# A two-layer transformer block on one core: attention scores of two 64-wide heads as two 64-row matmuls, units in pairs

## The chip, the cores and the metric

One core of one Trainium2 chip. The time is the device time of one launch in microseconds; the kernel before has three runs. The engines are called PE (TensorE: matmuls and transposes; PEld is its weight loads), DVE (VectorE), ACT (ScalarE), POOL (GpSimd) and SP (it only issues DMAs here).

## What is computed

512 latent tokens and 256 context tokens, 1024 wide, go through two layers in fp32. Each layer normalises and modulates the tokens, projects them once, and runs four groups of four heads side by side: A full attention with two key heads, B latent attention (keys 96 wide), C a window of 128 keys to either side with a sink, D a neighbourhood with a learned bias; all of them also look at the 256 context keys. Then an output projection, a residual, and a mixture of 64 experts of which each token takes 8.

```python
def _dense_block_attn(q, k, v, scale):
    ...
        s = jnp.einsum("bhgqd,bhkd->bhgqk", qi, k, preferred_element_type=jnp.float32) * scale
        p = jax.nn.softmax(s, axis=-1).astype(v.dtype)
        return jnp.einsum("bhgqk,bhkd->bhgqd", p, v)
...
    for l in range(DEPTH):
        with_ctx = l < DEPTH - 1
        ...
        mix = jnp.concatenate([oa, ob, ow, on], axis=-1) @ w_out[l]
        x = x + g1 * _rms_norm(mix, post_mix_g[l])
        ...
        f = _moe(tokens, router_w[l], router_b[l], exp_w_gate[l], exp_w_up[l], exp_w_down[l], ...)
```

In layer 0 the context tokens are updated too (they attend to context keys alone), in layer 1 not.

## The kernel before

`build` calls, for each layer, `norm_in`, four times `mixer` (groups A, B, C, D), `project_out`, then `route`, `experts` and `ffn_residual`. Each is a block with one instruction list per engine, written out by hand; between blocks all engines meet. Semaphores (`Signal`) order the engines within a block, and each engine works through its list in order. In the profile the tensors of a mixer carry its layer and group in their name: PR_0A, KT_1D.

A `mixer` has two parts. In the first, PE projects the six token tiles of 128 (`project`, L550) and turns queries and keys (`turn`, L571), so that QT and KT hold the width of a head in the partitions. In the second it works off **units**: one head for one tile of 128 queries, in the order head by head, tile by tile. There are 24 units in layer 0 (6 tiles: 4 latent, 2 context) and 16 in layer 1. For each unit:

- `scores` (PE, L581 and L582): queries against up to 512 latent keys and against 256 context keys, into one of two areas of PSUM, `pp[u % 2]`. Context units have the second product alone.
- `maximum` (DVE, L788; D first subtracts its bias, L782; C its masks, L785 and L787, and takes the sink in, L791): the scores are negated, so it is a minimum.
- `exps` (ACT, L670): exponentials and their sum, into PR.
- `turn_probs` (PE, L589): six transposes of 128 columns.
- two copies from PSUM into PT: the latent part on ACT (L680), the context part on DVE (L820).
- `values` (PE, L597): six products with V; behind them, in some units, two tiny products (L603) that finish a **piece** of the modulation vector.
- `divide` (DVE, L801 and L807, in C also L799; L804 for the piece): the result into o_tok.

The heads of A, C and D are 64 wide. KT holds two key heads one above the other, in partitions 0 to 63 and 64 to 127, and QT holds each query head in the half of its key head, the other half being zero (memset, L714). So a product over 128 rows gives the scores of one head. B has rows 0 to 95 filled and the rest zero.

The pieces are the work of POOL (`piece`, L512 to L515): 12 per mixer in layer 0 and 8 in layer 1, each 9.3 us long, multiplying and adding weights that SP loads two at a time (L498). Piece j goes with unit `unit_of[j]`, that is units 1, 3, 5 and so on up to the last; `values` of that unit waits for it. After 8 pieces POOL needs a slot that `values` has read.

The order on the engines, with u the unit:

```python
for u in range(NU):          # PE (between: scores(0) first, values(NU - 1) last)
    scores(u + 1); values(u - 1); turn_probs(u)
for u in range(NU):          # ACT, after exps(0)
    exps(u + 1); copy_latent(u)
for u in range(NU):          # DVE, after maximum(0)
    maximum(u + 1); divide(u - 1); copy_context(u)
```

`scores(u)` waits for the exponentials of u - 2, `turn_probs(u)` for those of u and for `divide(u - 2)`.

Of the kernel before, what the change touches and what calls it, by code (L numbers as in the profile page):

```python
# [27 lines left out]
P = 128  # L28
# [3 lines left out]
SEQ, CTX = 512, 256  # L32
LT, CT = SEQ // P, CTX // P
NT = LT + CT
HD = 64
# [9 lines left out]
NROW = NT * P  # L45
# [355 lines left out]
def mixer(v, l, g, nt, hT, wg, o_tok):  # L401
# [5 lines left out]
    isA, isB, isC, isD = (name == x for x in "ABCD")  # L407
# [12 lines left out]
    s_sc, s_max, s_exp, s_pt = S("scores"), S("negated_maximum"), S("exponentials"), S("probs_turned")  # L420
    s_pa, s_pd, s_pv, s_o, s_sx = S("probs_by_act"), S("probs_by_dve"), S("weighted_values"), S("out_written"), S("sink_exp")

    units = [(h, q) for h in range(4) for q in range(nt)]
    NU = len(units)

    def lo(u):

        q = units[u][1]
        if q >= LT:
            return 512  # L430
        if isC:
            return 512 - P * (min(q + 1, LT - 1) - max(q - 1, 0) + 1)
        return 0
# [17 lines left out]
    NP, NA = len(pieces), 8  # L451
# [3 lines left out]
    s_aw, s_as, s_acc = [S("ada_loaded0"), S("ada_loaded1")], S("ada_step"), S("ada_summed")  # L455
    s_mr, s_pad = S("mod_columns"), S("padded")

    steps, counts = [], []
    local = [sum(units[w][1] < LT for w in range(u + 1)) for u in range(NU)]

    with ExitStack() as scope:
# [20 lines left out]
        pp = [v.banks(0, 2), v.banks(2, 4)]  # L482
        tq, tk = ps[:, 4, :], ps[:, 5, :]

        with nc.Block() as block:  # L485
# [54 lines left out]
            @block.tensor  # L540
            def _(pe):
                def project(i):

                    s_rows.wait(pe, i - 1)
                    if not isB:
                        s_v.wait(pe, i - 1)
                    a = 0 if has_q[i] else kv0
                    for c0, c1 in ((a, min(W, 512)), (512, W)):
                        for k in range(KD if c1 > c0 else 0):
                            last = pe.matmul(pp[i % 2][:, c0:c1], hT[:, k, i * P:(i + 1) * P], wg[g % 2][:, k, c0:c1],  # L550
                                             start=(k == 0), stop=(k == KD - 1))
                    last.then_inc(s_proj.sem, 1)

                def latent(i):

                    s_cn.wait(pe, i + 1)
                    pe.transpose(ps[:, 7, 0:P], cn[:, i % 2, :], v.ident).then_inc(s_ct.sem, 1)
                    s_ce.wait(pe, i + 1)
                    s_kn.wait(pe, i)
                    pe.matmul(ps[:, 6, :], cT[:, i % 2, :], wup[:, :], start=True, stop=True).then_inc(s_up.sem, 1)  # L560

                def turn(i):
                    s_rows.wait(pe, i + 1)
                    if isB:
                        s_kn.wait(pe, i + 1)
                    s_qe.wait(pe, nq[i])
                    s_ke.wait(pe, i)
                    for j in range(0 if has_q[i] else NQ, NQ + NK):
                        dst, c = (tq, j) if j < NQ else (tk, j - NQ)
                        src = R[:, i % 2, j * KP:(j + 1) * KP]  # L570
                        last = pe.transpose(dst[0:KP, c * P:(c + 1) * P], src, v.ident)  # L571
                    last.then_inc(s_t.sem, 1)

                def scores(u):
                    s, q = units[u]
                    s_exp.wait(pe, u - 1)
                    kvp = s if isB else s // 2 if isD else 0
                    a, k0 = lo(u), key_tile(u, lo(u) // P) * P
                    lhs = QT[:, s, q * P:(q + 1) * P]
                    if a < 512:  # L580
                        pe.matmul(pp[u % 2][:, a:512], lhs, KT[:, kvp, k0:k0 + 512 - a], start=True, stop=True)  # L581
                    pe.matmul(pp[u % 2][:, 512:768], lhs, KT[:, kvp, SEQ:NROW], start=True, stop=True).then_inc(s_sc.sem, 1)  # L582

                def turn_probs(u):
                    s_exp.wait(pe, u + 1)
                    s_o.wait(pe, u - 1)
                    b = 4 + 2 * (u % 2)
                    for c in range(lo(u) // P, 6):
                        last = pe.transpose(ps[:, b + c // 4, (c % 4) * P:(c % 4 + 1) * P], PR[:, u % 2, c * P:(c + 1) * P], v.ident)  # L589
                    last.then_inc(s_pt.sem, 1)  # L590

                def values(u):
                    s_pa.wait(pe, local[u])
                    s_pd.wait(pe, u + 1)
                    c0 = kv_of(units[u][0]) * HD
                    for c in range(lo(u) // P, 6):
                        last = pe.matmul(ps[:, 5 + 2 * (u % 2), 256:256 + HD], PT[:, u % 2, c * P:(c + 1) * P],  # L597
                                         V[:, key_tile(u, c), c0:c0 + HD], start=(c == lo(u) // P), stop=(c == 5))
                    if u in piece_of:
                        j = piece_of[u]  # L600
                        s_acc.wait(pe, j + 1)
                        for c in range(2):
                            last = pe.matmul(ps[:, 5 + 2 * (u % 2), 320 + c:321 + c], acc[:, j % NA, c, :], v.ones[:, :],  # L603
                                             start=True, stop=True)
                    last.then_inc(s_pv.sem, 1)

                s_w.wait(pe, 16)
                if isB:
                    s_wup.wait(pe, 16)
                project(0)  # L610
                for i in range(NT):
                    if i + 1 < NT:
                        project(i + 1)
                    if isB:
                        latent(i)
                    turn(i)

                s_qe.wait(pe, nq[NT])
                s_ke.wait(pe, NT)
                s_pad.wait(pe, 2)  # L620
                if not isB:
                    s_v.wait(pe, NT)
                scores(0)
                for u in range(NU):
                    if u + 1 < NU:
                        scores(u + 1)
                    if u:
                        values(u - 1)
                    turn_probs(u)
                values(NU - 1)  # L630

            @block.scalar
            def _(act):
# [29 lines left out]
                def exps(u):  # L663
                    s_max.wait(act, u + 1)
                    s_pt.wait(act, u - 1)
                    a = lo(u)
                    if isC:
                        act.activation(st[:, 3, u:u + 1], small[:, S_SINK + units[u][0]:S_SINK + units[u][0] + 1], ACT.Exp,
                                       bias=st[:, 1, u:u + 1])
                    act.activation(PR[:, u % 2, a:768], pp[u % 2][:, a:768], ACT.Exp, bias=st[:, 1, u:u + 1], scale=-1.0,  # L670
                                   accum_out=st[:, 2, u:u + 1]).then_inc(s_exp.sem, 1)

                exps(0)
                for u in range(NU):
                    if u + 1 < NU:
                        exps(u + 1)
                    if lo(u) < 512:
                        s_pt.wait(act, u + 1)
                        s_pv.wait(act, u - 1)
                        act.copy(PT[:, u % 2, lo(u):512], ps[:, 4 + 2 * (u % 2), lo(u):512]).then_inc(s_pa.sem, 1)  # L680

            @block.vector
            def _(dve):
                n = [0]
# [23 lines left out]
                if isB:  # L708
                    dve.memset(QT[KP:P, :, :], 0.0).then_inc(s_pad.sem, 1)
                    dve.memset(KT[KP:P, :, :], 0.0).then_inc(s_pad.sem, 1)  # L710
                else:
                    for side in range(2):
                        rest = QT[(1 - side) * HD:(2 - side) * HD, :, :].rearrange("p (j s) n -> p j s n", s=2)
                        dve.memset(rest[:, :, side, :], 0.0).then_inc(s_pad.sem, 1)  # L714
                for i in range(NT):
                    tok = slice(i * P, (i + 1) * P)
                    pr = pp[i % 2]
# [92 lines left out]
                if isC:  # L810
                    step(dve.tensor_scalar(nsink[:, :], small[:, S_SINK:S_SINK + 4], -1.0, None, ALU.mult))
                maximum(0)
                for u in range(NU):
                    if u + 1 < NU:
                        maximum(u + 1)
                    if u:
                        divide(u - 1)
                    s_pt.wait(dve, u + 1)
                    s_pv.wait(dve, u - 1)
                    dve.tensor_copy(PT[:, u % 2, 512:768], ps[:, 5 + 2 * (u % 2), 0:256]).then_inc(s_pd.sem, 1)  # L820
                divide(NU - 1)
                steps.append(n[0])

# [4 lines left out]
        s.stage_over(k)  # L828
    for j in range(2):
        s_aw[j].stage_over(16 * ((NP + 1 - j) // 2))  # L830
    for s, k in ((s_as, counts[0]), (s_acc, NP), (s_pad, 2), (s_mr, NP)):
        s.stage_over(k)
    if not isB:
        s_v.stage_over(NT)
# [852 lines left out]
```

## Time and profile before

| | |
|---|---|
| runs | 3464.82, 3468.37, 3480.79 us (median 3468.37) |
| span of the profiled execution | 3472.4 us (the page gives no time of its own beside it) |
| PE, DVE, ACT, POOL busy | 87%, 37%, 18%, 33% |
| attention stretches of the eight mixers | 484.3 us of span in sum: PE 450.6 busy, DVE 304.2, POOL 389.1 |
| the eight mixers, projections included | 1070 us |
| experts | most of the rest |

The page's busy shares are averages over stages of different kind: the 142 expert blocks alone hold most of PE's time. What the change touches lies in eight stretches of 49 to 80 us each, so they are read by windows, and the engines' interplay by the timeline. A busy time is the sum of instruction durations; the number in brackets behind a row of the timeline is how long the engine stood idle before it, and what released it. An "x2" joins instructions of the same kind that follow each other. Each fp32 product is two LDWEIGHTS and two MATMUL records.

### The profile page before, as it was taken

How to read it: one execution, taken by the hardware profiler on the slowest of the kernel's cores; microseconds unless marked ns; L12 is line 12 of the kernel's file. 1: busy time of each engine (PE TensorE's matmuls, PEld its weight loads, DVE VectorE, ACT ScalarE, POOL GpSimd, SP SyncE). 2: the span in 40 equal slices, each digit the busy share in tenths (PEclk: the TensorE clock that was granted, in tenths of full speed). 3: DMA queues.
4: the chain of work that ended last, by engine and by line, in shares of the span. 5: the costliest groups of instructions: out<-in, count | busy, mean ns of one | idle time of the engine just before them, and what ended most of it. 6: DMA issues, size and time to landing. Idle time of an engine off the chain costs nothing. (4 is left out here: it accounts for less than half of the span.)

```text
span 3472.4 us, 54592 instructions
## 1 busy us (share of the span) xinstructions
PE 3025.3 (87%) x17979; PEld 2267.7 (65%) x17980; DVE 1300.4 (37%) x3937; ACT 617.2 (18%) x1376; POOL 1162.9 (33%) x1009
## 2 busy tenths in 40 slices
PE   6688979988899999989994698899789999999995
PEld 5365655636577777777773466666457777777774
DVE  5643461524333333323334644524322332233223
ACT  1122231310111111111113122212111111111111
POOL 0766798500121222212222637672111221222122
PEclk9898999997999999999997898999799999999998
DMA  6121212103589888898884211221359999988995
GB/s 218 31 70 37 85 49 96 62 27 112 214 252 322 263 251 287 284 306 272 286 276 141 67 53 31 85 88 39 114 184 312 300 310 295 300 273 245 300 304 161
DMA packets 199258, 642.71 MB, mean 185 GB/s; under 512 B 23296, under 2 KB 117760, under 8 KB 165632
## 3 DMA queue, kind: packets, MB, share of 16 engines
q1 hardware_dynamic: 157264, 520.86, 41.2%
q0 software_dynamic: 41904, 120.67, 16.9%
q8 instruction: 53, 0.87, 0.1%
q14 instruction: 37, 0.30, 0.0%
HBM read 589.19 MB, written 89.03 MB: 195 GB/s over the span
## 5 line engine op out<-in xcount | busy, mean ns | idle before, releaser
L1389 PEld LDWEIGHTS ps<-xT,wgu 128*128 128x128 f32 x9088 | 1033.3, 192 | 116.0 <-issue 115.2
L1389 PE MATMUL ps<-xT,wgu 128*128 128x128 f32 x9088 | 1048.1, 276 | 26.4 <-DVE xT L1473 24.2
L1337 POOL DMA_INDIRECT X<-h_rows,gix x146 | 149.2, 1022 | 1300.8 <-DVE wc L1476 659.5
L1396 PE MATMUL ps<-wd,hidden 128*128 128x512 f32 x1136 | 525.8, 606 | 0.0
L550 PE MATMUL ps<-w_in,hT 128*128 128x512 f32 (+3 forms) x1152 | 396.9, 505 | 15.6 <-PEq L485 4.3
L1396 PEld LDWEIGHTS ps<-wd,hidden 128*128 128x128 f32 x1136 | 209.3, 194 | 215.1 <-issue 212.3
L550 PEld LDWEIGHTS ps<-w_in,hT 128*128 128x128 f32 x1152 | 213.2, 203 | 184.9 <-issue 177.4
L1485 DVE TENSOR_TENSOR hidden<-silu,ps 128x128 f32<-128x128 f32 x284 | 81.5, 287 | 596.7 <-ACT silu L1441 595.4
L1356 POOL DMA_INDIRECT ffn_rows<-Y,six x142 | 226.4, 1595 | 170.8 <-ACT Y L1446 147.7
L1382 PE MATMUL ps<-cst,X 128*128 128x128 f32 x1152 | 162.3, 286 | 99.4 <-DMA X<-h_rows,gix 99.1
L1441 ACT ACTIVATE silu<-ps 128x128 f32<-128x128 f32 x284 | 78.7, 277 | 902.3 <-PE ps L1389 902.3
L1382 PEld LDWEIGHTS ps<-cst,X 128*128 128x128 f32 x1152 | 128.2, 144 | 106.5 <-DMA X<-h_rows,gix 106.2
L1446 ACT ACTIVATE Y<-ps,wc 128x512 f32<-128x512 f32 x142 | 97.6, 687 | 442.0 <-PE ps L1396 402.4
L1487 DVE COPY six<-gix 128x1 uint32<-128x1 uint32 x142 | 21.8, 153 | 344.2 <-DMA ffn_rows<-Y,six 344.0
L1498 DVE TENSOR_SCALAR Y<-ps,wc 128x512 f32<-128x512 f32 x142 | 106.4, 749 | 111.3 <-PE ps L1396 111.3
L906 PE MATMUL ps<-w_in,oT 128*128 128x512 f32 x320 | 139.3, 594 | 0.0
L1459 DVE TENSOR_SCALAR mark<-csth,cur 128x128 f16<-128x128 f16 x736 | 137.0, 271 | 5.2
L1435 ACT COPY xT<-ps 128x512 f32<-128x512 f32 x144 | 84.2, 585 | 246.3 <-PE ps L1382 246.3
L1455 DVE TENSOR_SCALAR cur<-gm,cst 128x6 f32 (+1 forms) x146 | 47.1, 322 | 168.1 <-issue 168.1
L906 PEld LDWEIGHTS ps<-w_in,oT 128*128 128x128 f32 x320 | 60.6, 191 | 73.0 <-issue 73.0
L1473 DVE COPY xT<-ps 128x512 f32<-128x512 f32 x144 | 98.0, 680 | 10.0 <-PE ps L1382 10.0
L930 POOL TENSOR_TENSOR mss<-mss,half 128x1 f32<-128x1 f32 x10 | 5.5, 548 | 204.7 <-DVE mss L954 204.7
(447 smaller groups left out, 3652.4 us busy)
## 6 DMA issues: line engine op xcount, KB each, us to landing
wgu<-in_exp_gu SPq DMA_DIRECT2D x128, 2048.0 KB, 8.9
wd<-in_exp_d SPq DMA_DIRECT2D x128, 1024.0 KB, 7.8
ada_start<-in_ada_w SPq DMA_DIRECT2D x8, 1024.0 KB, 9.7
w_in<-in_w_in SPq DMA_DIRECT2D x4, 2048.0 KB, 8.2
w_in<-in_w_out SPq DMA_DIRECT2D x4, 2048.0 KB, 11.1
aw_0A<-in_ada_w SPq DMA_DIRECT2D x12, 512.0 KB, 3.8
aw_0B<-in_ada_w SPq DMA_DIRECT2D x12, 512.0 KB, 3.9
w_in<-in_w_in SPq DMA_DIRECT2D x2, 3072.0 KB, 10.6
```

The source lines that it names most:

```text
L550: last = pe.matmul(pp[i % 2][:, c0:c1], hT[:, k, i * P:(i + 1) * P], wg[g % 2][:, k, c0:c1], start=(k == 0), stop=(k == KD - 1))
L906: last = pe.matmul(ps[:, 2 * (i % 2) + n, :], oT[:, i % 2, k, :], w[n][:, k, 0:512], start=(k == 0), stop=(k == KD - 1))
L1337: pool.indirect_dma_start(out=X[j][:, :], out_offset=None, in_=v.h2_dram, in_offset=bass.IndirectOffsetOnAxis(ap=gix[j][:, 0:1], axis=0), ...
L1356: pool.indirect_dma_start(out=v.acc_dram, out_offset=bass.IndirectOffsetOnAxis(ap=six[j][:, 0:1], axis=0), in_=Y[j][:, :], in_offset=None, ...
L1382: last = pe.transpose(ps[:, 3 + k // 4, (k % 4) * P:(k % 4 + 1) * P], X[j][:, k * P:(k + 1) * P], v.ident)
L1389: last = pe.matmul(ps[:, f, h * P:(h + 1) * P], wgu[w][:, k, h * FD + f * P:h * FD + (f + 1) * P], xT[:, k, :], start=(k == 0), stop=(k == ...
L1396: last = pe.matmul(ps[:, 5 + c, :], G[:, f, :], wd[w][:, f, c * 512:(c + 1) * 512], start=(f == 0), stop=(f == 1))
L1435: act.copy(xT[:, 0:4, :].rearrange("p k c -> p (k c)"), ps[:, 3, :]).then_inc(x_act, 1)
L1446: act.activation(Y[j][:, 0:512], ps[:, 5, :], ACT.Copy, scale=wc[j][:, 0:1]).then_inc(y_act, 1)
L1459: last = dve.tensor_scalar(mark[:, t, :], csth[:, H_IOTA:H_IOTA + P], cur[:, t:t + 1], None, ALU.is_equal)
L1473: dve.tensor_copy(xT[:, 4:8, :].rearrange("p k c -> p (k c)"), ps[:, 4, :]).then_inc(x_dve, 1)
L1498: dve.tensor_scalar(Y[j][:, 512:D], ps[:, 6, :], wc[j][:, 0:1], None, ALU.mult).then_inc(y_dve, 1)
```

## The change

Units are taken in pairs: heads 2j and 2j + 1 for the same tile. `scores_of_two` issues the wide product of both heads and then the narrow product of both; each reads only the 64 partitions that its head fills (B still reads 128). The two heads are in different halves of the array's rows and write to different areas of PSUM. QT's other halves are no longer set to zero, and PE's wait for the memsets goes, except in B. The order of the three engines within the attention part is new for all four groups.

```diff
-    units = [(h, q) for h in range(4) for q in range(nt)]
+    units = [(2 * j + s, q) for j in range(2) for q in range(nt) for s in range(2)]
...
-                def scores(u):
-                    s, q = units[u]
-                    s_exp.wait(pe, u - 1)
-                    kvp = s if isB else s // 2 if isD else 0
+                def scores_of_two(u):
+
+                    s_exp.wait(pe, u)
                     a, k0 = lo(u), key_tile(u, lo(u) // P) * P
-                    lhs = QT[:, s, q * P:(q + 1) * P]
-                    if a < 512:
-                        pe.matmul(pp[u % 2][:, a:512], lhs, KT[:, kvp, k0:k0 + 512 - a], start=True, stop=True)
-                    pe.matmul(pp[u % 2][:, 512:768], lhs, KT[:, kvp, SEQ:NROW], start=True, stop=True).then_inc(s_sc.sem, 1)
+                    for c0, c1, k in ((a, 512, k0), (512, 768, SEQ)):
+                        for w in range(2 if c0 < c1 else 0):
+                            s, q = units[u + w]
+                            side = slice(0, P) if isB else slice((s % 2) * HD, (s % 2 + 1) * HD)
+                            ins = pe.matmul(pp[w][:, c0:c1], QT[side, s, q * P:(q + 1) * P],
+                                            KT[side, s if isB else s // 2 if isD else 0, k:k + c1 - c0], start=True, stop=True)
+                            if c0 == 512:
+                                ins.then_inc(s_sc.sem, 1)
...
-                s_pad.wait(pe, 2)
-                if not isB:
+                if isB:
+                    s_pad.wait(pe, 2)
+                else:
                     s_v.wait(pe, NT)
-                scores(0)
-                for u in range(NU):
-                    if u + 1 < NU:
-                        scores(u + 1)
-                    if u:
-                        values(u - 1)
+                scores_of_two(0)
+                for u in range(0, NU, 2):
+                    if u + 2 < NU:
+                        scores_of_two(u + 2)
                     turn_probs(u)
-                values(NU - 1)
+                    turn_probs(u + 1)
+                    values(u)
+                    values(u + 1)
...
                 exps(0)
+                exps(1)
                 for u in range(NU):
-                    if u + 1 < NU:
-                        exps(u + 1)
                     if lo(u) < 512:
                         s_pt.wait(act, u + 1)
                         s_pv.wait(act, u - 1)
                         act.copy(PT[:, u % 2, lo(u):512], ps[:, 4 + 2 * (u % 2), lo(u):512]).then_inc(s_pa.sem, 1)
+                    if u % 2 == 1 and u + 1 < NU:
+                        exps(u + 1)
+                        exps(u + 2)
...
-                else:
-                    for side in range(2):
-                        rest = QT[(1 - side) * HD:(2 - side) * HD, :, :].rearrange("p (j s) n -> p j s n", s=2)
-                        dve.memset(rest[:, :, side, :], 0.0).then_inc(s_pad.sem, 1)
...
                 maximum(0)
+                maximum(1)
                 for u in range(NU):
-                    if u + 1 < NU:
-                        maximum(u + 1)
-                    if u:
+                    if u % 2 == 0 and u:
+                        divide(u - 2)
                         divide(u - 1)
+                    if u + 2 < NU:
+                        maximum(u + 2)
                     s_pt.wait(dve, u + 1)
                     s_pv.wait(dve, u - 1)
                     dve.tensor_copy(PT[:, u % 2, 512:768], ps[:, 5 + 2 * (u % 2), 0:256]).then_inc(s_pd.sem, 1)
+                divide(NU - 2)
                 divide(NU - 1)
```

On PE, in the midst of 1D's attention (scores L581 and L582, values L597, piece L603, turns L589), two units stand before as

```order
L581 MATMUL ps<-KT_1D,QT_1D 128x512
L582 MATMUL ps<-KT_1D,QT_1D 128x256
L597 MATMUL ps<-V_1D,PT_1D 128x64 x6
L603 MATMUL ps<-ones,aacc_1D 128x1 x2
L589 MATMUL ps<-cst,PR_1D 128x128 x6
L581 MATMUL ps<-KT_1D,QT_1D 128x512
L582 MATMUL ps<-KT_1D,QT_1D 128x256
L597 MATMUL ps<-V_1D,PT_1D 128x64 x6
L589 MATMUL ps<-cst,PR_1D 128x128 x6
```

and in the changed kernel, where L582 is both score products, L592 the turns, L600 the values and L606 the piece, as

```order
L582 MATMUL ps<-KT_1D,QT_1D 128x512 x2
L582 MATMUL ps<-KT_1D,QT_1D 128x256 x2
L592 MATMUL ps<-cst,PR_1D 128x128 x12
L600 MATMUL ps<-V_1D,PT_1D 128x64 x12
L606 MATMUL ps<-ones,aacc_1D 128x1 x2
```

The values of a unit stood one unit behind its turns, with the next scores between them; now both follow at once, and nothing stands between the second turns and the values.

On DVE at the same place, before (bias L782, minimum L788, L801 to L807 the division, L820 the copy), two units:

```order
L782 TENSOR_TENSOR ps<-ps,TD_1D 128x512
L788 TENSOR_REDUCE st_1D<-ps 128x1
L801 RECIPROCAL st_1D<-st_1D 128x1
L804 TENSOR_SCALAR mod_raw<-ps,small 128x2
L807 TENSOR_SCALAR o_tok<-ps,st_1D 128x64
L820 COPY PT_1D<-ps 128x256
L782 TENSOR_TENSOR ps<-ps,TD_1D 128x512
L788 TENSOR_REDUCE st_1D<-ps 128x1
L801 RECIPROCAL st_1D<-st_1D 128x1
L807 TENSOR_SCALAR o_tok<-ps,st_1D 128x64
L820 COPY PT_1D<-ps 128x256
```

and in the changed kernel (bias L784, minimum L790, division L803 to L809, copy L824):

```order
L803 RECIPROCAL st_1D<-st_1D 128x1
L809 TENSOR_SCALAR o_tok<-ps,st_1D 128x64
L803 RECIPROCAL st_1D<-st_1D 128x1
L806 TENSOR_SCALAR mod_raw<-ps,small 128x2
L809 TENSOR_SCALAR o_tok<-ps,st_1D 128x64
L784 TENSOR_TENSOR ps<-ps,TD_1D 128x512
L790 TENSOR_REDUCE st_1D<-ps 128x1
L824 COPY PT_1D<-ps 128x256
L784 TENSOR_TENSOR ps<-ps,TD_1D 128x512
L790 TENSOR_REDUCE st_1D<-ps 128x1
L824 COPY PT_1D<-ps 128x256
```

The divisions of a pair stand together ahead; the copy of the second unit stands behind the bias and minimum of the second unit of the next pair.

## Rows read from the trace of the kernel before

**Rows 1.** The page's head.

```profile
span 3472.4 us, 54592 instructions
```

**Rows 2.** Stretches (attention of 0A, 0C, 1A, 1D): PE, PEld, DVE, ACT, POOL busy; PEclk.

```profile
150.00:216.00 66.00, 63.94 (x407) 50.41 (x408) 35.21 (x90) 28.09 (x60) 61.61 (x57) 0.96 0.20 57
447.70:515.00 67.30, 53.47 (x344) 42.20 (x345) 53.25 (x156) 25.68 (x79) 62.67 (x60) 0.97 0.19 56
1979.60:2035.00 55.40, 54.58 (x350) 44.09 (x350) 28.53 (x66) 23.93 (x47) 39.40 (x37) 0.96 0.10 29
2338.50:2395.00 56.50, 54.07 (x350) 42.46 (x350) 38.71 (x82) 23.53 (x47) 28.53 (x28) 1.00 0.07 20
```

**Rows 3.** Timeline of 1A: start, length, engine, line, what [idle before, releaser].

```profile
1993.04 1.02 PE L581 MATMUL ps<-KT_1A,QT_1A 128*128 128x512 f32 x2
1994.34 1.45 PE L597 MATMUL ps<-V_1A,PT_1A 128*128 128x64 f32 x12
1994.54 0.96 DVE L788 TENSOR_REDUCE st_1A<-ps 128x1 f32<-128x768 f32 x1 [0.87 <-PE ps L582]
1995.53 0.90 ACT L670 ACTIVATE PR_1A<-ps,st_1A 128x768 f32<-128x768 f32 x1 [1.70 <-DVE st_1A L788]
1995.62 0.83 PE L589 MATMUL ps<-cst,PR_1A 128*128 128x128 f32 x6
1996.28 1.02 PE L581 MATMUL ps<-KT_1A,QT_1A 128*128 128x512 f32 x2
1996.33 0.19 ACT L670 ACTIVATION_READ_ACCUMULATOR PR_1A<-ps,st_1A 128x1 f32 x1
1996.48 0.58 ACT L680 COPY PT_1A<-ps 128x512 f32<-128x512 f32 x1
1996.48 0.42 DVE L820 COPY PT_1A<-ps 128x256 f32<-128x256 f32 x1 [0.18 <-PE ps L589]
1998.86 0.56 PE L603 MATMUL ps<-ones,aacc_1A 128*128 128x1 f32 x4
1999.97 0.60 PE L581 MATMUL ps<-KT_1A,QT_1A 128*128 128x512 f32 x1
```

**Rows 4.** Timeline of 1D, two units.

```profile
2354.09 1.02 PE L581 MATMUL ps<-KT_1D,QT_1D 128*128 128x512 f32 x2
2355.58 0.70 DVE L782 TENSOR_TENSOR ps<-ps,TD_1D 128x512 f32<-128x512 f32 x1 [0.82 <-PE ps L582]
2355.59 1.42 PEld L597 LDWEIGHTS ps<-V_1D,PT_1D 128*128 128x128 f32 x12 [0.45 <-ACT PT_1D L680]
2361.33 1.02 PE L581 MATMUL ps<-KT_1D,QT_1D 128*128 128x512 f32 x2
```

**Rows 5.** Timeline: the last piece on POOL and on PE, 0A to 0D.

```profile
228.18 0.45 POOL L515 TENSOR_TENSOR aacc_0A<-atmp_0A 128x128 f32<-128x128 f32 x1
228.68 1.02 PE L603 MATMUL ps<-ones,aacc_0A 128*128 128x1 f32 x4 [2.33 <-POOL aacc_0A L515]
396.17 0.45 POOL L515 TENSOR_TENSOR aacc_0B<-atmp_0B 128x128 f32<-128x128 f32 x1
397.08 0.96 PE L603 MATMUL ps<-ones,aacc_0B 128*128 128x1 f32 x4
523.71 0.45 POOL L515 TENSOR_TENSOR aacc_0C<-atmp_0C 128x128 f32<-128x128 f32 x1
525.52 0.96 PE L603 MATMUL ps<-ones,aacc_0C 128*128 128x1 f32 x4
654.51 0.45 POOL L515 TENSOR_TENSOR aacc_0D<-atmp_0D 128x128 f32<-128x128 f32 x1
676.97 0.96 PE L603 MATMUL ps<-ones,aacc_0D 128*128 128x1 f32 x4
```

**Rows 6.** Timeline: start of 0A's mixer on DVE.

```profile
72.82 1.34 DVE L714 MEMSET QT_0A<- 64x1536 f32 x1 [0.79 <-PEq L294]
```

**Rows 7.** Timeline: first scores of 1A.

```profile
1979.66 2.04 PE L581 MATMUL ps<-KT_1A,QT_1A 128*128 128x512 f32 x2 [0.43 <-DVE KT_1A L772]
```

More of the change, by code:

```diff
@@ L830, in mixer @@
         s_aw[j].stage_over(16 * ((NP + 1 - j) // 2))
-    for s, k in ((s_as, counts[0]), (s_acc, NP), (s_pad, 2), (s_mr, NP)):
+    for s, k in ((s_as, counts[0]), (s_acc, NP), (s_pad, 2 if isB else 0), (s_mr, NP)):
         s.stage_over(k)
```

## The prediction

> **What bounds the kernel now.** The page gives the span of the profiled execution [rows 1], 3472.4 us, and no time outside it; the median of the runs is 3468.37. The sum below is a difference against the profiled execution, which stands 0.1% above the median. Only the attention part of eight mixers is touched: 0A to 0D with 24 units each (a unit is one head of one 128-token tile), 1A to 1D with 16. The table by stretches [rows 2] shows PE busy for 98 to 99% of 0A's and 1A's attention, 96% of 1D's, and 79% of 0C's, where DVE has as much work. So PE seems to be the bound, and the timeline of 1A [rows 3] shows a unit's parts: the scores take 1.30 us (1993.04 to 1994.34), the weighted values 1.28 (to 1995.62), the six turns of the probabilities 0.66 (to 1996.28). Two units take 6.93 (1993.04 to 1999.97): twice 3.24, and 0.45 for the piece of modulation that every second unit adds. In 1D [rows 4] two units take 7.24 (2354.09 to 2361.33), since the weights of the values wait 0.45 for ACT.
>
> Two things beside PE matter. First POOL: it sums the modulation pieces, and the last unit of each mixer waits for the last of them. The ends of the mixers [rows 5] show 0A's last piece on POOL done at 228.63 and PE waiting 2.33 us for it; in 0B POOL is done at 396.62, PE's last product starts at 397.08; in 0C 524.16 and 525.52; only in 0D (654.96 against 676.97) and in layer 1 has POOL long been done. POOL's work is unchanged and hardly waits for attention. Second, the chain around PE: minimum on DVE 1.50 us after the scores start, exponentials, turn, two copies 0.86 after the turn starts, values [rows 3]. Before, each step has one unit's work as cover.
>
> **The change, part by part.**
>
> *The memsets* of QT's empty halves [rows 6] are dropped from DVE: 2 x 1.34 us while PE projects; the first result of that projection is there 8 us later. Worth 0.
>
> *The scores in halves of the array* (A, C, D). The arithmetic is as before, 4 matmul records per unit (two passes per product), 0.43 us for 512 columns, 0.22 for 256. No row shows two matmuls in different halves, so the price of a pair's scores lies between 2.60 us (one after the other, 2 x 1.30) and 1.30 (completely together). I take a value between: the two passes of one head use the same half and must follow each other, and matmuls start in the order of the program; so only the second pass of one head runs beside the first pass of the other. That gives 3 x 0.43 for the wide products, in whose last 0.43 the first head's two narrow passes fit, and 2 x 0.22 more: 1.73.
>
> *The new order, A.* PE does scores of both next units, two turns, two values; DVE does minimum, copy, minimum, copy; ACT both copies, then both exponentials. Counted from the start of the scores: first minimum 1.50 to 2.46; turns 1.73 to 3.05; copies can start at 2.59 and 3.25. DVE: copy to 3.01, second minimum to 4.00, second copy to 4.45. ACT: copies to 3.84, exponentials (0.90 + 0.19 each) to 6.04. PE: values 3.3 to 4.6, second values to 5.9, piece to 6.35. So a pair takes 6.35 where it took 6.93: 0.58 less, eight pairs 4.6. The start is dearer: the second pair's scores and the first turns wait for two minima and the second exponential, which ends 4.6 after the first scores start (1.50 + 0.99 + 0.99 + 1.12), while PE has 1.73 of work: 2.9 idle. Before, the first turns waited for one exponential, which ends at 3.6 with 2.6 of scores ahead: 1.0 idle. The 1.9 more, less 0.87 for the cheaper scores and what is saved at the last pair, I take as 0.6. 1A: -4.0.
>
> *B* keeps 128 rows and gets only the order. The first minimum starts at 2.35 (three products stand ahead of it), turns 2.60 to 3.92, ACT's copy ends at 4.05, values from 4.2, the end at 7.23: 0.30 more than 6.93. 1B: +2.4.
>
> *D* has the bias subtraction (0.70, 0.73 with its gap [rows 4]) ahead of each minimum, and the copy that the second values wait for stands behind both: 1.50 + 0.73 + 0.99 + 0.45 + 0.73 + 0.99 + 0.45 = 5.84, then 0.1 to restart, values 1.30, piece 0.45: 7.69. That is 0.45 more than 7.24 in the seven cycles from pair to pair, so 1D is +3. In 0D the latent pairs lose as much, the four context pairs gain (their scores shrink from 0.86 to 0.65, and they stand together): 0.
>
> *C* is between: DVE has masks, a second small minimum and one step more per unit. I take +1 for 1C (ends -2 and +4, the gain of A and the loss of D).
>
> *0A, 0B, 0C.* POOL's end stays: 0A cannot end earlier (0), 0B by 0.5 at most (0), 0C by 1.4 at most (-1). Were POOL faster, the cover of 0A's gain would be gone and some 4 us would appear.
>
> *The clock.* The first scores of 1A run at 1.2 GHz (2.04 us for two passes, against 1.02) [rows 7]; four tiny matmuls at the end of 0A take 1.02 against 0.56 [rows 3, 5], after PE had waited. More waiting at starts and in context pairs may keep the lower level a little longer: +1 over all.
>
> Sum over 0A to 0D and 1A to 1D: 0 + 0 - 1 + 0 - 4.0 + 2.4 + 1 + 3, and 1 for the clock: **+2**, with some 8 us either way if 0.1 us per pair is wrong in my chains (80 pairs). Against the median that is **3470 us**. What PE saves (0.87 us in most of the 60 pairs of A, C and D) goes to three places: POOL's end, the queue on DVE, and the starts.
>
> The Trainium skill ("TensorE: Matmul & The Clock Gate", Part 3) says that small matmuls in different row groups start some 4 ns apart and run together; no run here shows it. By it a pair's scores would take 1.30; the A pair would then be held by ACT's exponentials at 6.2, so the sum hardly moves.
>
> **The rivals.**
>
> 1. *The halves don't run together* (slower). Then the pair's scores take 2.60, the first minimum starts at 2.35, A pairs take 7.2 like B, D pairs 5.84 + 0.85 + 1.85 = 8.5. 1A +2, 1B +2, 1C +1, 0C -1, 0D +6 (eight latent pairs at +1.3, context pairs giving some back), 1D +9, clock +1: +20, 3488. For it: fp32 runs in two passes, and no row shows a pass beside another. Against it: different rows, different banks of PSUM. It decides from the point at which the overlap is under a third.
>
> 2. *Going from 128 rows to 64 and back empties the array.* The last of a row of 512-wide matmuls is shown 0.16 us longer than its spacing (1.02 for two at 0.43) [rows 3], so two switches cost 0.32 per pair. In the 36 pairs of 0D, 1A, 1C and 1D that is 12 at most, about 7 where DVE's chain covers one of the two: 3476. The Trainium skill ("TensorEngine Tiling (Array Packing)", Key Properties) states that a change of tiling mode drains TensorE. No run here shows it; it speaks against the change.
>
> 3. *PE alone decides* (faster). If the chain through DVE has more slack than I count, what PE saves is the gain: 8 x 0.87 each in 1A and 1D, 8 x 0.75 in 1C, about 8 in 0D: 28, so 3440. For it: 98% busy [rows 2]. Against it: in 1D the cycle is over 7.24 with PE busy for 6.9.
>
> 4. *The clock falls in the midst of attention*, because PE now waits in each pair. A pair of 6 us of PE work then takes some 10: +3 us and more in each of 80 pairs, over 3700. Against it: 0C ran with PE busy 79% at 0.97 [rows 2].
>
> **How the numbers follow.** A measurement of this kernel tells about 0.5% (17 us: under 3451 or over 3486) from no change. The forecast has 0.62, rival 1 0.16, rival 2 0.12, rival 3 0.06, rival 4 0.04. Forecast and rival 2 are the same within 0.5%, and rival 1, at 3488, lies at the bound: a fifth of it counts as same. Faster 0.06, same 0.77, slower 0.17. The range goes from 3457 (the forecast with its chains 8 better and 5 for the spread of the runs) to 3489 (rival 1); it leaves out rivals 3 and 4.
>
> **What would show it.** In the timeline of the changed kernel: scores records of a pair 0.43 apart with the second head's first pass starting with the first head's second; 1A about 4 us shorter with some 6.3 per pair; 1D with 7.6 to 7.7 and PE idle ahead of the second values, waiting for DVE's copy; 1B at 7.2; PE at 0A's last piece waiting 5 us or more for POOL and the mixer ending at the same time as before. D pairs at 7.0 or less, 0A ending early, or B pairs under 6.9 would prove me wrong; scores of 2.6 per pair would prove rival 1.

## The result and the profile after

The changed kernel takes 3498.12 us (median of 4 runs, 3495.89 to 3507.59) against 3474.0 for the kernel before on the same chips: a ratio of 1.0081 (95% interval [1.0056, 1.0106], as in all brackets behind a ratio below), 0.8% slower. The profiled execution has a span of 3505.4 us against 3472.4 [rows 1]. It is the slowest of the four runs: it shows 33.0 us more, where the medians differ by 24.1. The mean granted clock of the whole kernel is 0.923 to 0.925 in all four; the runs of the kernel before beside the first experiments have 0.936 to 0.941. The page:

```profile
span 3505.4 us, 54574 instructions
PE 3036.0 (87%) x17979; PEld 2279.0 (65%) x17980; DVE 1272.2 (36%) x3925; ACT 614.1 (18%) x1376; POOL 1164.4 (33%) x1009
PEclk9888979896899999999997898889799999999998
```

The stretches from the first scores to the last piece, after (columns as in [rows 2], whose stretches are shorter; 0A to 0D, then 1A to 1D):

```profile
150.50:229.70 79.20, 66.95 (x463) 53.86 (x464) 37.61 (x105) 29.24 (x65) 73.25 (x68) 0.87 0.16 47
324.80:405.00 80.20, 74.92 (x463) 59.63 (x464) 37.88 (x105) 28.01 (x64) 70.20 (x66) 0.95 0.16 47
454.80:538.90 84.10, 71.92 (x392) 58.05 (x392) 59.64 (x177) 28.02 (x88) 71.35 (x67) 0.70 0.16 45
609.40:693.20 83.80, 69.22 (x464) 56.25 (x464) 48.32 (x121) 28.78 (x64) 54.65 (x51) 0.90 0.11 32
1996.40:2053.10 56.70, 53.55 (x384) 43.68 (x384) 27.83 (x69) 23.70 (x48) 39.40 (x37) 0.90 0.10 29
2135.80:2200.80 65.00, 62.64 (x383) 49.33 (x384) 28.32 (x69) 23.70 (x48) 36.21 (x35) 0.93 0.09 25
2241.30:2307.50 66.20, 57.36 (x311) 47.16 (x311) 44.32 (x125) 22.30 (x64) 44.84 (x43) 0.69 0.11 32
2367.80:2434.80 67.00, 55.38 (x383) 43.87 (x384) 38.17 (x85) 24.57 (x48) 30.46 (x29) 0.92 0.06 17
```

Before, the same eight stretches lasted 550.7 us in sum; now 582.2, which is 31.5 of the span's 33.0. Only 1A is shorter. The column to look at is the granted clock (1.00 is TensorE's full 2.4 GHz, 0.50 its low level of 1.2 GHz): 0.69 and 0.70 in 1C and 0C, where it was 0.98 and 0.96.

All runs in one table: length of each stretch, its clock behind it. There is one profile of each. Where the clock stays high, mixers of equal code agree within about 1 us. Where it falls they do not: 0C with the code of before takes 78.4, 91.1 (c_as_before), 79.2 and 78.3 (the last two rows), and 1C with the changed code 66.2 and, with light POOL, 59.9.

```
                    0A        0B        0C        0D         1A        1B        1C        1D
before           79.2 .93  76.3 .95  78.4 .96  79.7 .97   60.3 .96  60.7 .96  55.0 .98  61.1 1.0
changed          79.2 .87  80.2 .95  84.1 .70  83.8 .90   56.7 .90  65.0 .93  66.2 .69  67.0 .92
order_only       80.3 .95  80.2 .95  81.8 .90  94.2 .88   65.0 .94  64.9 .94  64.0 .89  79.9 .85
halves_only     142.2 .50  75.9 .97 118.0 .50 142.5 .50  118.0 .50  60.7 .96  91.6 .51 117.2 .50
halves_filled    98.1 .96  75.7 .97  92.6 .91 102.4 .92   78.1 .95  60.3 .96  63.9 1.0  77.7 .96
copies_first     79.2 .87  79.6 .95  78.6 .79  79.7 .87   56.7 .90  65.0 .93  57.3 .82  63.1 .89
turns_first      79.3 .87  77.5 .95  91.7 .67  80.1 .87   55.2 .93  61.8 .97  68.1 .70  58.5 .97
c_as_before      79.3 .87  80.2 .95  91.1 .76  82.0 .93   56.6 .90  65.0 .93  55.0 .97  66.9 .90
c_filled         79.3 .87  80.3 .95  78.8 .89  87.0 .85   56.7 .90  65.0 .93  60.3 .92  68.4 .88
light_pool chg.  72.0 .90  80.2 .95  80.5 .76  83.9 .90   55.6 .92  65.0 .94  59.9 .80  71.8 .81
light_pool bef.  76.7 .95  75.0 .97  76.3 .89  80.0 .97   60.7 .96  60.3 .96  54.2 .98  61.1 1.0
best_of_each     79.2 .89  75.7 .97  79.2 .94  77.2 .91   55.1 .93  60.2 .97  54.9 .96  61.3 .92
pieces_moved     74.9 .84  76.3 .95  78.3 .96  77.5 .91   55.1 .93  60.4 .96  53.9 1.0  60.0 .94
```

The timeline of 1A after, PE, one pair:

```profile
2023.54 1.56 PE L582 MATMUL ps<-KT_1A,QT_1A 64*128 64x512 f32 x8
2025.04 1.53 PE L592 MATMUL ps<-cst,PR_1A 128*128 128x128 f32 x12
2026.59 2.89 PE L600 MATMUL ps<-V_1A,PT_1A 128*128 128x64 f32 x24
2029.31 0.56 PE L606 MATMUL ps<-ones,aacc_1A 128*128 128x1 f32 x4
2029.80 1.56 PE L582 MATMUL ps<-KT_1A,QT_1A 64*128 64x512 f32 x8
```

The scores of two units last 1.50 us (2023.54 to 2025.04). The halves run together: 2 x 0.43 + 2 x 0.22 is 1.30, and I put the other 0.20 down to the changes of rows. The Trainium skill ("TensorE: Matmul & The Clock Gate", Part 3) says that matmuls in different row groups run at the same time and start some 4 ns apart. The trace agrees in fp32: the single records of this pair show each pass of the second head 6 to 7 ns behind that of the first. The pair takes 6.26 (2023.54 to 2029.80). In 1D two pairs, PE, the first with its scores at the low clock and the second at the full:

```profile
2390.20 2.81 PE L582 MATMUL ps<-KT_1D,QT_1D 64*128 64x512 f32 x8
2395.20 1.52 PE L600 MATMUL ps<-V_1D,PT_1D 128*128 128x64 f32 x12 [0.34 <-DVE PT_1D L824]
2397.13 1.52 PE L600 MATMUL ps<-V_1D,PT_1D 128*128 128x64 f32 x12 [0.41 <-DVE PT_1D L824]
2398.98 1.56 PE L582 MATMUL ps<-KT_1D,QT_1D 64*128 64x512 f32 x8
2406.51 1.56 PE L582 MATMUL ps<-KT_1D,QT_1D 64*128 64x512 f32 x8
```

8.78 us for the first (2390.20 to 2398.98), 7.53 for the second (7.24 before [rows 4]). In the first pair PE waits for DVE's copy ahead of both values; in the second, the first wait is 0.73 for ACT's copy. At 0A's end PE waits 5.15 us for POOL's last piece (2.33 before [rows 5]):

```profile
229.06 1.01 PE L606 MATMUL ps<-ones,aacc_0A 128*128 128x1 f32 x4 [5.15 <-POOL aacc_0A L515]
```

### The profile page after: what moved, and what is told of

It reads as the page before. It is cut to its first block and busy times, and to the rows that moved or that the text cites. A ratio compares the mean times of both kernels' runs of the same rounds, so it can differ in the third digit from the quotient of the medians.

```text
span 3505.4 us, 54574 instructions
## 1 busy us (share of the span) xinstructions
PE 3036.0 (87%) x17979; PEld 2279.0 (65%) x17980; DVE 1272.2 (36%) x3925; ACT 614.1 (18%) x1376; POOL 1164.4 (33%) x1009
```

## The experiments

Three theories, of which more than one can hold. Theory W (waits): the new waits of PE bring the clock down. Theory H (halves): the 64-row scores do, since they keep less of the array at work. Theory Q (queue): the copy queued behind DVE's minimum holds the values.

**order_only** (`side = slice(0, P)` in `scores_of_two`, memsets kept).

> The changed kernel's order, but the scores of A, C and D again over all 128 rows with QT's other half zero. Theory W (waiting): the clock falls in 0C and 1C because PE stands still in every pair under the new order; then it falls here too, 1C has a mean granted clock near 0.7 and lasts over 64 us from the first scores to the last piece (55.0 before, 66.2 after the change), and the kernel is 30 us or more over the one before. Theory H (halves): it falls because the 64-row scores keep the engine less busy in the chip's eyes; then 1C here has a clock above 0.93 and lasts 56 to 58, and the kernel is about 18 us over the one before (from my chains with the scores in series: 1A +2.4, 1B +2.4, 1C +1, 0D +6, 1D +9, 0C -3). Both: pair scores last 2.6 us, 1A some 62 to 63 us against 60.3 before, 1D some 70 against 61.1.

Measured: 1.0188 [1.0162, 1.0215], 61 us more in the median (W asked for 30 or more, H for 18). 1C has 0.89 and 64.0 us: the new order lowers the clock by itself, but to 0.69 only with the halves. In 1D it is the other way round, 0.85 here and 0.92 with the halves. The pairs' scores last 2.67, as expected. 1D takes 79.9 where I expected 70: its pairs take 8.42 at the full clock, and three in a row have their scores at the low one and take 9.9 to 10.0, though no wait inside them is over 0.47:

```profile
2384.67 2.83 PE L582 MATMUL ps<-KT_1D,QT_1D 128*128 128x512 f32 x8
2393.09 4.41 PE L582 MATMUL ps<-KT_1D,QT_1D 128*128 128x512 f32 x8
2402.98 4.52 PE L582 MATMUL ps<-KT_1D,QT_1D 128*128 128x512 f32 x8
2412.99 4.52 PE L582 MATMUL ps<-KT_1D,QT_1D 128*128 128x512 f32 x8
2422.99 2.83 PE L582 MATMUL ps<-KT_1D,QT_1D 128*128 128x512 f32 x8
```

Shorter scores leave PE more time to wait, so the halves could have worked through the waits. In C the traces speak against it: behind the start, PE's waits in 1C sum to 5.1 us in the changed kernel (none over 0.9) and to 6.7 in the kernel before (up to 1.5, at a clock of 0.98). A slower PE waits less, so this alone is no proof; the next run is.

**halves_only** (the kernel before, `lhs = QT[side, ...]` and `KT[side, ...]` over 64 partitions).

> The order of before, with each unit's scores over the 64 rows its head fills (the two heads not next to each other). Theory H: the clock falls in 1C, 0C and 1D though no wait is added; 1C longer by 5 us or more. Theory W: the clock stays as before (0.96 to 1.00), and each unit costs only the change from 128 to 64 rows and back: 0.12 + 0.2 us as the changed kernel's pairs show around their scores, so 1A and 1D grow by 16 x 0.33 = 5 us each, 0D by up to 8, 1C by 3, 0A to 0C by less since POOL ends them; some +20 us in all. If that price is not paid, +0.

Measured: 1.0906 [1.0876, 1.0935], 310 us more. 1A:

```profile
2138.00:2256.00 118.00, 116.65 (x384) 84.63 (x384) 29.73 (x69) 25.14 (x48) 39.31 (x37) 0.50 0.05 14
```

PE is busy for 99% and yet at 1.2 GHz from end to end; so are all stretches of A, C and D (0.50 and 0.51), and not those of B (0.97 and 0.96), whose code is as before. Nothing but the 64 rows is different. That is H, and far beyond the 5 us that I had asked of it.

**halves_filled** (halves_only, and in `turn_probs` of A, C, D three times `pe.matmul(ps[:, b + 1, 384:512], v.ident, v.ident)`: full-width products whose result nobody reads).

> The old order with 64-row scores (1A 118 us, clock 0.50), with three 128-row products of 128 columns added per unit in A, C and D. If 64-row products merely fail to hold the clock up, the added full-width work brings it back in part: clock above 0.8 and 1A near 16 x (3.46 + 0.33 + 0.66) = 71 us, shorter than 118 although work was added. If they pull it down whatever stands beside them, the clock stays 0.50 and 1A lasts 118 + 21 = 139.

Measured: 3558.61 us in one run, 225 less than halves_only, with 720 more passes of 128 columns (an estimate of 79 us, at half of the 0.22 of a 256-column pass). 1A:

```profile
2030.20:2108.30 78.10, 76.75 (x480) 59.53 (x480) 29.72 (x69) 25.23 (x48) 39.29 (x37) 0.95 0.07 21
```

So 64-row products fail to hold the clock up; full-width work among them brings it back. The changes from 128 rows to 64 and back are all still there, so they alone do not bring it down.

1A takes 78.1 where I expected 71: that sum of 16 units left out the start and the end of the stretch, 4.9 us of the 60.3 before. The run also gives a price for the changes of rows. One unit at the full clock:

```profile
2050.28 0.89 PE L590 MATMUL ps<-cst 128*128 128x128 f32 x6
2051.01 0.82 PE L592 MATMUL ps<-cst,PR_1A 128*128 128x128 f32 x6
2051.75 1.12 PE L582 MATMUL ps<-KT_1A,QT_1A 64*128 64x512 f32 x2
2053.24 1.55 PE L600 MATMUL ps<-V_1A,PT_1A 128*128 128x64 f32 x12
2054.63 0.56 PE L606 MATMUL ps<-ones,aacc_1A 128*128 128x1 f32 x4
2055.05 0.91 PE L590 MATMUL ps<-cst 128*128 128x128 f32 x6
```

Without the added products (0.73) and the piece (0.42) the unit takes 3.62, against 3.24 before [rows 3]: 0.38 more.

**c_filled** (changed kernel, the same three products ahead of the second turns, in C).

> The changed kernel with three 128-row products of 128 columns added ahead of each pair's second turns, in C alone: 0.66 us more work of PE per pair at 2.4 GHz, 5 us in 1C. If the clock is what C lost (H or W), the granted clock in 1C rises from 0.69 to above 0.9 and 1C lasts 62 or less in spite of the added work (66.2 without it). If the clock is only a symptom of waits whose length is set elsewhere, 1C lasts 71 or more.

Measured: 1C 60.3 us at 0.92, 5.9 less with 5 added; 0C 5.3 less at 0.89. So the clock was C's loss. (The added products also fill some of PE's waits, so this run does not tell H from W.) The total, 1.0098 [1.0070, 1.0125], is no better than the changed kernel's: in the profiled run 0D, whose code is unchanged, took 3.2 more at 0.85.

```profile
2231.10:2291.40 60.30, 50.35 (x359) 42.65 (x360) 42.92 (x125) 21.99 (x64) 44.88 (x43) 0.92 0.13 36
```

**c_as_before** (changed kernel with C's order and rows as before).

> The changed kernel with only the C mixers as before (order and 128 rows). If 0C and 1C lose by their own mixture of halves and waits, they last 78 and 55 again and the kernel is 17 us under the changed one (5.7 + 11.2), some 3481. If the clock in C falls because of what runs ahead of it, they stay above 82 and 62.

Measured: 1.0061 [1.0038, 1.0084], some 7 us under the changed kernel's ratio where I expected 17, and the two intervals overlap. 1C is back at 55.0. But 0C, whose program is now the one before, took 91.1 at 0.76. Its clock can fall with 128-row scores and without any change of its own; why it did here is open. So the 5.7 us that 0C lost in the changed kernel cannot be put down to its own halves with certainty.

**copies_first** (DVE: `maximum` of the second unit behind `tensor_copy`).

> The changed kernel with DVE doing both context copies of a pair ahead of the second minimum of the next pair. Theory Q (the queue on DVE holds the second values): 1D's cycle falls from 7.53 to some 6.9 us, 1D to 61 to 62 us from first scores to last piece (67.0 in the changed kernel, 61.1 before), 0D by some 4, 1C by 2 or more; in sum 12 us or more less than the changed kernel. Against it: if the clock alone is what was lost, the waits only move to ACT's exponentials and the gain is under 5 us.

Measured: 1.0043 [1.0023, 1.0062]. 1D's pairs take 6.95 at the full clock (expected 6.9), and both values follow each other without a wait: Q holds. 0D and 1D are 4 us shorter; 1D, at 63.1, stays over the 61 to 62 expected, since one pair is at the low clock. 1C is 9 us shorter with its clock at 0.82 instead of 0.69, so part of that is the clock and not the queue. One edit in DVE's order gives back about half of the loss, by the two ratios; their intervals just touch.

**turns_first** (PE: turns, then `scores_of_two(u + 2)`, then values; DVE: copies, then both minima).

> The changed kernel with the turns of a pair ahead of the scores of the next pair, so that the scores stand between the turns and the values as cover for the copies, and both copies ahead of both minima on DVE. Theory Q: no wait of PE ahead of the values; 1D some 2 us under before, 1A 5 under (55), 0D 5 under; about 12 us less than the changed kernel at equal clock. Theory W adds: with fewer waits of PE the clock in 1C stays above 0.9 and another 8 to 12 us come back. Theory H: 1C's clock stays near 0.7.

Measured: 1.0063 [1.0036, 1.0089], which the intervals do not tell from the changed kernel. 1A (55.2) and 1D (58.5, pairs 6.85) are as expected. 0D is not: 80.1, no better than before, where I expected 5 less. C, at 0.67 and 0.70, took 13 more than before. That does not settle W, because the edit did not take C's waits away: it moved them. In 1C PE now waits for divisions ahead of the turns, 7.9 us in sum against 5.1 in the changed kernel, and for up to 2.16 at a time:

```profile
2245.27 0.74 PE L592 MATMUL ps<-cst,PR_1C 128*128 128x128 f32 x5 [2.16 <-DVE o_tok L809]
2271.91 1.30 PE L592 MATMUL ps<-cst,PR_1C 128*128 128x128 f32 x5 [2.11 <-DVE o_tok L809]
```

**best_of_each** (A and D as in turns_first, B and C as before).

> A and D in pairs with 64-row scores and the turns ahead of the next scores, B and C exactly as before. By the runs so far 1A lasts 55.2 (60.3 before), 1D 58.5 (61.1), 0D about 80 (79.7), B and C as before, 0A held by the last piece: 8 us under the kernel before, some 3466, which the interval may not tell from it. If C's fall of the clock spills over from A and B and is not C's own, 1C stays above 60 and nothing is won.

Measured: 0.9977 [0.9959, 0.9996], 12 runs, 8 us less in the median, as expected: a gain of 0.2% that the interval just tells from nothing. Inside it the parts fell otherwise: 0D took 77.2 (expected 80), 1D 61.3 at 0.92 (expected 58.5). Both C mixers kept their clock (0.94, 0.96) behind the paired A.

**light_pool_before, light_pool_changed** (without the two additions `tmp[:, 0:half] + tmp[:, half:2 * half]`; the modulation is then another, tokens are routed otherwise, so only the mixers compare; one run each).

> The kernel before with the same additions on POOL left out. Its 0A waited 2.33 us for the last piece, so 0A lasts 76 to 77 instead of 79.2. Together with the run on the changed kernel this gives what the change is worth in 0A once POOL is out of the way: 2 to 3 us by this reckoning, 4 to 5 by 1A's example (twice eight pairs alike); nothing if 0A is held by something else.

> The changed kernel with POOL's two intermediate additions per piece left out (part of the modulation sum is missing), so that a piece takes about half as long and no mixer waits for the last one. If POOL's last piece is what ends 0A (5.15 us of waiting there), 0A lasts 73 to 75 us from first scores to last piece instead of 79.2; 0B and 0C change by under 1 us at equal clock; layer 1 not at all.

Measured: 0A 76.7 before and 72.0 changed. With POOL light the change is worth 4.7 us in 0A, with POOL as it is nothing. 0A of the changed kernel came out 1 us under the 73 to 75 expected. 0C fell by 3.6 at 0.76, where I expected under 1 at equal clock, and 1D took 71.8 at 0.81, 4.8 more than in the changed kernel: with the same program on PE and DVE, the clock of C and D moved their times by more than the steps that I had forecast there.

**best_with_pieces_moved** (best_of_each with `share = (11, 12, 12, 13)` pieces for layer 0: one of 0A's pieces goes to 0D).

> The best-of-each kernel with one of 0A's twelve pieces moved to 0D, where POOL is done 20 us early. If POOL ends 0A, 0A gets 4 to 5 us shorter (75) and 0D stays; some 4 us under the best-of-each kernel, 12 under the one before (3460). If PE would be no earlier, 0A stays 79.

Measured: 3454.46 us, 0.9955 [0.9933, 0.9977]; 0A 74.9 (expected 75) and 0D 77.5, as in best_of_each. It beats both kernels, the one before by 0.45%.

## Why the prediction was wrong

The forecast was 3470, no change, in 3457 to 3489; measured 3498, slower by 0.8%. Term by term (us, stretches of the profiles):

```
            0A     0B     0C     0D     1A     1B     1C     1D
forecast     0      0     -1      0   -4.0   +2.4     +1     +3    and +1 for the clock
measured     0   +3.9   +5.7   +4.1   -3.6   +4.3  +11.2   +5.9
```

- ***The clock*, "+1 over all", is the step that failed.** 1C and 0C lost 11.2 and 5.7 where I had +1 and -1. In c_filled a clock of 0.92 and 0.89 instead of 0.69 and 0.70 gives back 5.9 and 5.3 in spite of added work. In 1D, of +5.9, the full-clock pairs explain some 2 (seven times 0.29), two pairs with scores at 1.2 GHz like the one above another 2.5, and the rest is the start, whose second scores run at 1.2 GHz too. I took the clock of 0C, 0.97 at 79% busy, as proof that a PE with waits keeps it, in rival 4 too. That row was of 128-row work in the old order; with 64 rows the busy share no longer speaks for the clock, as halves_only shows (99% busy, 0.50). Rival 4 had the right mechanism. Its reason, the waits, is at most part of it: in order_only the new order alone brings 1D to 0.85 and 1C to 0.89. Its size (every pair of all mixers) was wrong. How much of C's fall in the changed kernel is due to the rows and how much to the order stays open, and 0C in c_as_before fell with neither.
- *0B and 0D* I put at 0. For 0B I had a chain of +0.30 a pair and did not use it, as if POOL's end were a lid with time under it for PE. But PE's last product stood only 0.46 behind POOL's end [rows 5]. The eight latent pairs took 0.38 more each, 3.0 in sum, and 0B ran over by 3.9. 0D's loss is again the clock for the most part: in four of its pairs the scores or the turns run at the low level and take 2.5 to 2.9 us instead of 1.6.
- *Scores in halves*: I took 1.73 per pair; measured 1.50. I had ruled that only the second pass of one head runs beside the first of the other; both passes run side by side.
- *Pairs at the full clock*: A 6.26 (forecast 6.35), B 7.31 (7.23), D 7.53 (7.69), rival 1's D 8.42 in order_only (8.5). The chains were right to 0.2 us, and 1A came out 3.6 shorter (forecast 4.0). 1B's seven cycles explain 2.7 of its +4.3; the rest lies at its two ends, for which I had put nothing. My reading that PE is busy for 98 to 99% of 0A's attention is a little high: 63.94 of 66.00 is 97% [rows 2].
- *POOL ends 0A*: right, to the us (79.2 both times; 4.7 us hidden).
- *Rival 2*: changes of rows do cost time on PE's path, some 0.2 per pair of units in the changed kernel, and 0.38 per unit in halves_filled, where each unit changes twice. The rule of the Trainium skill ("TensorEngine Tiling (Array Packing)", Key Properties) that a change of mode drains TensorE fits that; no run here shows the draining itself.

## What to carry to other kernels

Count what a cheaper step does to the granted clock before counting its saving. Zero rows in a product are not only waste here, they come with the full clock: with 64-row scores issued one head at a time, attention took up to twice as long (1A 118.0 for 60.3). Two heads side by side kept 0.87 to 0.92 in A and D, but 0.70 in C. When steps are taken in pairs, look for the copy that now stands behind the next pair's long instruction. And a saving on PE is worth nothing in a mixer that another engine's last piece ends, until that piece is moved.

## What was not expected

A stretch with PE 99% busy sat at 1.2 GHz for 118 us (0.50), and some 79 us (the estimate above) of added full-width products shortened the kernel by 225. The fall does not need long waits: in 1D of the changed kernel no wait inside the pairs was over 0.74 us. What decides between 0.69 in C and 0.92 in D stays open, and so does why 0C fell to 0.76 in c_as_before with the code of the kernel before.
